# Even mixer of a two-layer decoder trunk: index scores in groups beside x_b, gate units in blocks beside nine pairs of the attention, LRU factors on Pool

## The chip, the cores and the metric

The kernel is one program on one core of a Trainium2 chip. The core has five engines that run their own instruction streams and meet only at semaphores: TensorE (PE in the profile; PEld is its weight load), VectorE (DVE), ScalarE (ACT), GpSimd (POOL) and SyncE (SP, which here only issues transfers). The metric is the device time of one launch in microseconds (us), lower is better.

## The reference

The trunk works on h (512 tokens x 1024 channels, float32). Each of two layers adds a half-step FFN, a mixer, a cross-attention to 256 memory tokens and a second half-step FFN. The change lies in the mixer of layer 0, the even mixer:

```python
q, c_kv, q_i, k_i, w_i, gate_b, x_b = _split(h @ w_in, EVEN_SPLITS)   # 512,256,512,64,8,512,512
c_kv = rmsnorm(c_kv, kv_norm); k = c_kv @ w_uk; v = c_kv @ w_uv       # 8 heads of 64
# index scores, 8 index heads of 64; the top 128 keys of each query are kept
sc = einsum('bqhd,bsd->bqhs', q_i, k_i) * IDX_DIM ** -0.5
score = where(causal, einsum('bqhs,bqh->bqs', relu(sc), w_i * IDX_HEADS ** -0.5), -inf)
_, idx = top_k(score, 128)
a_out = softmax over the kept keys of (q @ k^T * 64 ** -0.5), times v
# RG-LRU on the other 512 channels
xc = causal_dwconv(x_b, conv_w, conv_b)                               # 4 taps
r = sigmoid(xc @ w_ra + b_ra); i = sigmoid(xc @ w_ri + b_ri)
log_a = -8 * r * softplus(-lam); a = exp(log_a)
b = sqrt(-expm1(2 * log_a)) * (i * xc)
b_out = scan(h_t = a_t * h_{t-1} + b_t) * gelu(gate_b)
return concat([a_out, b_out]) @ w_out
```

## The kernel before

Weights come as a stream of units of 128 x 1024 float32 (512 KB). SP loads unit v into one of two raw buffers when unit v-2 has been split; ACT writes the rounded high part (`split_hi`, L334) and DVE the low part (`split_lo`, L339), and PE multiplies high by high, high by low and low by high (`three`, L354 to L356, or `streamed`, L1592 to L1594). A unit of a projection is 8 blocks of three matmuls with 512 columns. Four slots hold split units, so a split is written 4 units ahead (`AHEAD`) of the one being drained. `w_ready` counts units that are split, `w_free` those that PE has used, `p_free` projection tiles copied out of PSUM.

The order of work in `even` is written out by hand on each engine; nothing is scheduled. Before the change it is, on PE:

- q_idx, c_kv, and the unit with the index keys and weights; then 24 index scores (L1789: three query blocks of 8 heads, with 256, 384 and 512 columns, in float32, two passes each). They go to PSUM banks 2 and 3 in turn, each waiting for the `relu` (ACT, L801) of the one two before.
- x_b (4 units), uk (1), uv (1), gate (4), then 8 LRU gate products (L1814), then q (4).
- the attention (`attend`, 32 steps, 8 heads of 4 query tiles t with (t+1)*128 keys): score (L1822) into bank 0 or 1; DVE adds the selection mask `e_sc` and takes the row maximum (L1161) and scales it (L1164); ACT takes the exponential (L687); DVE multiplies by the reciprocal of the sum (L1171, L1172); PE transposes the probabilities two steps later (L1636); DVE copies them to `e_pT` (L1179); after each head PE mixes with v (L1830), ACT and DVE split the result (L705, L1148). `recurrence` puts the LRU factors, their products and the scan between these steps on DVE.
- the output projection (`output`, L1592 to L1594, 8 units).

On DVE each index score is accumulated into `e_sc` (L1287, L1291), with the norm of c_kv between (`latent`: L1256 to L1272). Then follows the selection: 48 rounds, each of MAX8 (L1305), which finds the 8 largest, and MATCH_REPLACE8 (L1306), which marks them, 16 rounds for each of the three query blocks. Four rounds stand behind each of the 14 splits from x_b to q. On Pool: one causal fill for each query block, then the convolution of the four x_b tiles (L433 to L438: one tensor_scalar and six tensor_tensor for each), then i * xc (L445).

## Time and profile before

| | us |
|---|---|
| runs of the kernel, median (lowest to highest) | 2417.82 (2417.5 to 2418.16), 3 runs |
| the profiled execution | 2417.31 |
| its span in the trace | 2415.5 |
| PE, DVE, ACT, POOL busy | 2328.6, 1024.7, 843.6, 48.0 |
| mean granted clock of TensorE | 0.97 |

The profiled execution is 0.51 us below the median; 1.8 us of it lie outside the span. Times in the trace count from the start of the span. "Granted clock" is the share of full speed that TensorE was given: 1.00 is 2.4 GHz and 0.50 is 1.2 GHz. Matmuls overlap in the pipeline, so the pitch of a stream is read from the starts of its rows, not from the duration of one. The even mixer from its index scores on stands between 429 and 651 us; PE is near fully busy at full clock almost everywhere else.

### The profile page before, as it was taken

The page shows a single profiled execution, that of the slowest core. Times are in us where ns is not written, and L with a number is a line of the kernel's source. Part 1 is how long each engine was busy: PE and PEld are TensorE (multiplying, and loading weights), DVE is VectorE, ACT ScalarE, POOL GpSimd, SP SyncE. Part 2 cuts the span into 40 slices and gives each one's busy share as a digit, 9 for nine tenths or more (in the row PEclk, how much of TensorE's full clock was granted, in tenths as well). Part 3 has the DMA queues.
Part 4 walks back from the last instruction along what each step waited for, and adds up shares of the span by engine and source line. Part 5 has one row for each costly group of instructions (what it writes and reads, how often), then busy time and mean ns, then how long its engine had stood idle before and what let it go on. Part 6 is the DMA issues. An engine that isn't in the chain of part 4 may idle for free.

```text
span 2415.5 us, 28776 instructions
## 1 busy us (share of the span) xinstructions
PE 2328.6 (96%) x10808; PEld 1886.4 (78%) x10808; DVE 1024.7 (42%) x1544; ACT 843.6 (35%) x1343; POOL 48.0 (2%) x54
## 2 busy tenths in 40 slices
PE   7999999997899999999999999999988999999998
PEld 7888888573487788888888888888757877888887
DVE  4333235697563453333253333243364535333322
ACT  4222224353253443222243222244433534322321
POOL 0000000240000000000000000000000000000000
PEclk9999999796799999999999999999999999999999
DMA  4222332120134213323223223323203412233232
GB/s 157 96 96 96 105 113 83 42 78 21 44 105 131 78 63 105 100 95 109 96 87 105 96 96 106 99 86 105 84 30 105 148 63 86 87 96 100 96 101 87
DMA packets 61938, 221.83 MB, mean 92 GB/s; under 512 B 7952, under 2 KB 8080, under 8 KB 61856
## 3 DMA queue, kind: packets, MB, share of 16 engines
q1 hardware_dynamic: 57024, 207.64, 26.7%
q10 hardware_dynamic: 4832, 13.03, 1.6%
q8 instruction: 59, 0.97, 0.2%
q14 instruction: 23, 0.19, 0.0%
HBM read 218.55 MB, written 2.10 MB: 91 GB/s over the span
## 4 chain that ended last, share of the span: by engine, by line
PE 90%; DVE 7%; issue 2%; ACT 1%; DMA 0%; SPq 0%; DVEq 0%; ACTq 0%
PE ps L354 17%; PE ps L356 17%; PE ps L355 17%; PE ps L1592 10%; PE ps L1594 10%; PE ps L1593 10%; DVE e_sc L1306 1%; PE ps L1702 1%; PE ps L1711 1%; DVE e_max L1305 1%; PE ps L1493 1%; PE ps L1830 1%; DVE w_lo L339 1%; PE ps L1789 1%; PE ps L1822 0%
## 5 line engine op out<-in xcount | busy, mean ns | idle before, releaser
L354 PE MATMUL ps<-x_hi,w_hi 128*128 128x512 f32 (+1 forms) x2016 | 753.4, 374 | 11.5 <-issue 9.4
L355 PE MATMUL ps<-x_lo,w_hi 128*128 128x512 f32 (+1 forms) x2016 | 747.6, 371 | 0.0
L356 PE MATMUL ps<-x_hi,w_lo 128*128 128x512 f32 (+1 forms) x2016 | 747.4, 371 | 0.0
L339 DVE TENSOR_TENSOR w_lo<-w_raw,w_hi 128x1024 fp32r<-128x1024 f32 x194 | 242.3, 1252 | 544.9 <-ACT w_hi L334 544.0
L354 PEld LDWEIGHTS ps<-x_hi,w_hi 128*128 128x128 f32 x2016 | 383.0, 190 | 80.2 <-issue 16.1
L355 PEld LDWEIGHTS ps<-x_lo,w_hi 128*128 128x128 f32 x2016 | 383.1, 190 | 65.1 <-issue 1.2
L356 PEld LDWEIGHTS ps<-x_hi,w_lo 128*128 128x128 f32 x2016 | 382.7, 190 | 64.6
L350 DVE TENSOR_TENSOR w_lo<-w_raw,w_hi 128x1024 fp32r<-128x1024 f32 x176 | 215.8, 1226 | 291.5 <-ACT w_hi L345 291.5
L334 ACT ACTIVATE w_hi<-w_raw 128x1024 fp32r<-128x1024 f32 x194 | 204.8, 1057 | 374.5 <-PE ps L1594 304.7
L345 ACT ACTIVATE w_hi<-w_raw 128x1024 fp32r<-128x1024 f32 x176 | 186.2, 1058 | 280.8 <-PE ps L356 275.6
L1592 PE MATMUL ps<-w_hi,act_hi 128*128 128x512 f32 x608 | 236.5, 389 | 0.0
L1593 PE MATMUL ps<-w_lo,act_hi 128*128 128x512 f32 x608 | 236.5, 389 | 0.0
L1594 PE MATMUL ps<-w_hi,act_lo 128*128 128x512 f32 x608 | 236.5, 389 | 0.0
L1077 DVE TENSOR_TENSOR tmp<-ps,tmp 128x512 f32<-128x512 f32 x88 | 60.9, 692 | 315.1 <-ACT tmp L603 315.1
L603 ACT ACTIVATE tmp<-ps 128x512 f32<-128x512 f32 x88 | 52.8, 600 | 370.2 <-PE ps L356 370.2
L1592 PEld LDWEIGHTS ps<-w_hi,act_hi 128*128 128x128 f32 x608 | 114.1, 188 | 23.8
L1593 PEld LDWEIGHTS ps<-w_lo,act_hi 128*128 128x128 f32 x608 | 114.1, 188 | 23.7
L1594 PEld LDWEIGHTS ps<-w_hi,act_lo 128*128 128x128 f32 x608 | 114.1, 188 | 23.5
L1592 PE MATMUL ps<-w_hi,x_hi 128*128 128x512 f32 x192 | 76.4, 398 | 6.0 <-DVE x_lo L1462 4.5
L1593 PE MATMUL ps<-w_lo,x_hi 128*128 128x512 f32 x192 | 75.8, 395 | 0.0
L1594 PE MATMUL ps<-w_hi,x_lo 128*128 128x512 f32 x192 | 75.7, 394 | 0.0
L1081 DVE TENSOR_TENSOR act_lo<-tmp,act_hi 128x512 f32 x88 | 60.2, 684 | 0.0
(280 smaller groups left out, 2250.7 us busy)
## 6 DMA issues: line engine op xcount, KB each, us to landing
w_raw<-in_wstream SPq DMA_DIRECT2D x390, 512.0 KB, 3.5
gain_bc<-in_gains ACTq DMA_DIRECT2D x8, 512.0 KB, 4.5
tmp<-in_post_gains ACTq DMA_DIRECT2D x8, 512.0 KB, 4.5
c_mem<-in_mem ACTq DMA_DIRECT2D x2, 1024.0 KB, 4.8
out_dram<-h SPq DMA_DIRECT2D x4, 512.0 KB, 2.6
h<-in_x SPq DMA_DIRECT2D x2, 512.0 KB, 6.1
h<-in_x ACTq DMA_DIRECT2D x2, 512.0 KB, 7.5
c_gain<-in_mem_gains ACTq DMA_DIRECT2D x2, 512.0 KB, 6.0
```

The costliest lines, as they stand in the source:

```text
L334: nc.scalar.activation(weights(v)[0], w_raw[:, v % 2, :], ACT.Copy).then_inc(w_hi_ready, 1)
L339: nc.vector.tensor_tensor(wl, w_raw[:, v % 2, :], wh.bitcast(f32), ALU.subtract).then_inc(w_ready, 1)
L345: nc.scalar.activation(weights(like)[0], w_raw[:, like % 2, :], ACT.Copy).then_inc(w_hi_ready, 1)
L350: nc.vector.tensor_tensor(wl, w_raw[:, like % 2, :], wh.bitcast(f32), ALU.subtract).then_inc(w_ready, 1)
L354: nc.tensor.matmul(dst, wh, xh, start=start, stop=False)
L355: nc.tensor.matmul(dst, wh, xl, start=False, stop=False)
L356: return nc.tensor.matmul(dst, wl, xh, start=False, stop=stop)
L1077: nc.vector.tensor_tensor(tmp[:, jj, :], bank(2 * jj + 1), tmp[:, jj, :], ALU.mult)\
L1081: nc.vector.tensor_tensor(act_lo[:, bass.ds(j, 1), :], tmp[:, jj:jj + 1, :], act_hi[:, bass.ds(j, 1), :].bitcast(f32), ALU.subtract)\
L1592: nc.tensor.matmul(dst, ah, wh, start=start, stop=False)
L1593: nc.tensor.matmul(dst, ah, wl, start=False, stop=False)
L1594: return nc.tensor.matmul(dst, al, wh, start=False, stop=stop)
```

## The change

- **Unit order.** In the stream q now comes before gate. SP has ten transfers written out for this stretch, with `stream_unit` giving the place in the unchanged array, between two loops.
- **Index scores.** `IN_FRONT = (2, 6, 5, 5, 5, 5, 4)`: of the 32 blocks of x_b, so many stand before each group of four scores, and four behind the last. The scores use four banks (2, 3, 5, 6). On ACT and DVE the copies and splits that x_b brings stand after n = 3, 11, 19; on DVE three selection rounds each stand after n = 11, 15, 19, 23.
- **Selection.** The other 36 rounds stand behind the splits at x_b 3, uk, uv, q 0, q 1, q 2 (8, 6, 6, 6, 5, 5).
- **LRU.** The 8 gate products go in as 6 behind q 1 and 2 behind q 2. The five factor steps per tile (with one more instruction, six) and the two products before the scan move from DVE to Pool; Pool's fills stand between its convolutions. The gelu and the product with it stand after the attention, the square root after pair 7.
- **Attention.** 16 pairs m of two steps. The key projection is copied with scale -1/8 and the mask is +3e38 for excluded keys, so that DVE's min is the bias itself: the small scaling instruction and its wait are gone. `e_p` has six slots. The copy of the transposed probabilities goes from DVE to ACT. `BESIDE = (4, 4, 4, 4, 4, 3, 3, 3, 3)`: the 32 blocks of gate stand beside pairs 0 to 8. From pair 10 on, even pairs write banks 6 and 7, odd ones 0 and 1.
- **Output.** The first two of the 8 output units are started tile by tile (`out_tile`) while the last head and the gelu are under way.

On PE at the start of the index scores, before:

```order
L1776 MATMUL ps<-tmp,ones 128x512 [waits e_sq] x2
L1780 MATMUL ps<-ident,e_wi 128x8 [waits p_free]
L1780 MATMUL ps<-ident,e_wi 128x8 x3
L1789 MATMUL ps<-e_k,e_qi 128x256 [waits e_w]
L1789 MATMUL ps<-e_k,e_qi 128x256
L1789 MATMUL ps<-e_k,e_qi 128x256 [waits e_relu] x6
L1789 MATMUL ps<-e_k,e_qi 128x384 [waits e_relu] x8
L1789 MATMUL ps<-e_k,e_qi 128x512 [waits e_relu] x8
L354 MATMUL ps<-x_hi,w_hi 128x512 [waits w_ready,p_free]
```

The same place after (L1800 is the index score, L356 to L358 are a block of x_b):

```order
L356 MATMUL ps<-x_hi,w_hi 128x512 [waits w_ready,p_free,e_w]
L357 MATMUL ps<-x_lo,w_hi 128x512
L358 MATMUL ps<-x_hi,w_lo 128x512
L356 MATMUL ps<-x_hi,w_hi 128x512
L357 MATMUL ps<-x_lo,w_hi 128x512
L358 MATMUL ps<-x_hi,w_lo 128x512
L1800 MATMUL ps<-e_k,e_qi 128x256 [waits e_w]
L1800 MATMUL ps<-e_k,e_qi 128x256 x3
L356 MATMUL ps<-x_hi,w_hi 128x512
```

Blocks of x_b now stand before and between the scores, and the first four scores wait for no relu.

On DVE in the accumulation of the index scores, before:

```order
L1287 TENSOR_SCALAR e_sc<-tmp,e_w 128x384 [waits e_relu,stat_link]
L1291 SCALAR_TENSOR_TENSOR e_sc<-tmp,e_w,e_sc 128x384 [waits e_acc,e_relu] x2
L1267 SCALAR_TENSOR_TENSOR e_ck<-e_ck,col,e_t 128x512
L1291 SCALAR_TENSOR_TENSOR e_sc<-tmp,e_w,e_sc 128x384 [waits e_acc,e_relu] x3
```

The same place after (L1301 and L1302 are a selection round, L341 the low part of a weight unit):

```order
L1313 TENSOR_SCALAR e_sc<-tmp,e_w 128x384 [waits e_relu,stat_link]
L1317 SCALAR_TENSOR_TENSOR e_sc<-tmp,e_w,e_sc 128x384 [waits e_acc,e_relu] x2
L1277 SCALAR_TENSOR_TENSOR e_ck<-e_ck,col,e_t 128x512
L1317 SCALAR_TENSOR_TENSOR e_sc<-tmp,e_w,e_sc 128x384 [waits e_acc,e_relu]
L341 TENSOR_TENSOR w_lo<-w_raw,w_hi 128x1024 [waits w_hi_ready]
L1301 MAX e_max<-e_sc 128x8 [waits e_filled]
L1302 MATCH_REPLACE e_sc<-e_max,e_sc 128x256 [waits stat_link]
L1301 MAX e_max<-e_sc 128x8 [waits stat_link]
```

A split and three rounds now stand between accumulations; the first round waits for Pool's fill, which stands behind Pool's first convolution.

On PE in the attention, before (L1822 score, L1636 transposition, L1830 mix):

```order
L1822 MATMUL ps<-e_kT,e_qT 128x256 [waits at_sm]
L1636 MATMUL ps<-ident,e_p 128x128 [waits at_pT,at_p]
L1636 MATMUL ps<-ident,e_p 128x128 x3
L1822 MATMUL ps<-e_kT,e_qT 128x384 [waits at_sm]
L1636 MATMUL ps<-ident,e_p 128x128 [waits at_pT,at_p]
L1830 MATMUL ps<-e_pT,e_v 64x512 [waits at_pT]
```

After, around pair 0 (L1844 is the score):

```order
L1844 MATMUL ps<-e_kT,e_qT 128x128 [waits e_sig,p_free]
L1844 MATMUL ps<-e_kT,e_qT 128x256
L356 MATMUL ps<-x_hi,w_hi 128x512 [waits w_ready,p_free]
L357 MATMUL ps<-x_lo,w_hi 128x512
L358 MATMUL ps<-x_hi,w_lo 128x512
L356 MATMUL ps<-x_hi,w_hi 128x512
```

Scores stand in pairs, and four blocks of gate stand between a pair's scores and the transpositions of the pair before.

The diff, cut to its core:

```diff
-    "even": [("q_idx", 4), ("c_kv", 2), ("kw_idx", 1), ("x_b", 4), ("uk", 1), ("uv", 1), ("gate", 4), ("q", 4),
+    "even": [("q_idx", 4), ("c_kv", 2), ("kw_idx", 1), ("x_b", 4), ("uk", 1), ("uv", 1), ("q", 4), ("gate", 4),
...
+        gate_bank = (2, 3, 4, 5, 6, 7, 2, 3)
+        index_bank = (2, 3, 5, 6)
+        NOT_CAUSAL, TAKEN, MASKED = -3.4e38, -3.2e38, 3.0e38
+
+        IN_FRONT = (2, 6, 5, 5, 5, 5, 4)
+        BESIDE = (4, 4, 4, 4, 4, 3, 3, 3, 3)
...
+        def score_bank(step):
+
+            m = step // 2
+            return bank((6 if m > len(BESIDE) and m % 2 == 0 else 0) + step % 2)
...
+                conv(0)
+                fill(1)
+                conv(1)
+                fill(2)
+                conv(2)
+                fill(3)
+                conv(3)
                 for c in range(LRUT):
-                    pool.wait_ge(e["sig"], 2 * LRUT)
-                    nc.gpsimd.tensor_tensor(e_xc[:, c, :], e_xc[:, c, :], f_i[:, c, :], ALU.mult)\
-                        .then_inc(e["t2"], 1)
+                    T, R, Z = f_r[:, c, :], tmp[:, c, :], e_t[:, c % 2, :]
+                    pool.wait_ge(e["sig"], LRUT + c + 1)
+                    nc.gpsimd.tensor_tensor(e_xc[:, c, :], e_xc[:, c, :], f_i[:, c, :], ALU.mult).then_inc(e["t2"], 1)
+                    pool.wait_ge(e["tanh"], c + 1)
+                    link(nc.gpsimd.tensor_scalar(R, R, 0.5, 0.5, ALU.mult, ALU.add))
+                    link(nc.gpsimd.tensor_tensor(Z, T, R, ALU.mult))
+                    link(nc.gpsimd.tensor_tensor(Z, Z, R, ALU.add))
+                    link(nc.gpsimd.tensor_scalar(Z, Z, -1.0, 2.0, ALU.mult, ALU.add))
+                    link(nc.gpsimd.tensor_tensor(R, R, Z, ALU.mult))
+                    pool.wait_ge(e["t2"], c + 1)
+                    nc.gpsimd.tensor_scalar(f_i[:, c, :], R, 2.0, -1.0, ALU.mult, ALU.add).then_inc(e["bv"], 1)
+                for c in range(LRUT):
+                    pool.wait_ge(e["sqrt"], c + 1)
+                    link(nc.gpsimd.tensor_tensor(tmp[:, c, :], f_r[:, c, :], tmp[:, c, :], ALU.mult))
+                    nc.gpsimd.tensor_tensor(e_xc[:, c, :], tmp[:, c, :], e_xc[:, c, :], ALU.mult)\
+                        .then_inc(e["prod"], 1)
...
+                    if n % 8 == 3:
+                        project_one("x_b", n // 8, e_xb, CONV - 1)
+                project_one("x_b", 3, e_xb, CONV - 1)
...
+                for m in range(N // 2 + 1):
+                    if m < N // 2:
+                        for step in (2 * m, 2 * m + 1):
+                            c, w = step % 4 * 4, (step % TT + 1) * P
+                            act.wait_ge(at_sm, a0 + step + 1)
+                            nc.scalar.activation(e_p[:, step % 6, 0:w], e_p[:, step % 6, 0:w], ACT.Exp,
+                                                 bias=e_st[:, c:c + 1], scale=-1.0,
+                                                 accum_out=e_st[:, c + 2:c + 3]).then_inc(at_e, 1)
+                    if m < len(BESIDE):
+                        done = [sum(BESIDE[:n]) // UB for n in (m, m + 1)]
+                        for j in range(*done):
+                            project_one("gate", j, e_gate)
+                    if m == 7:
+                        act.preload_act_table(ACT.Sqrt)
                         for c in range(LRUT):
+                            act.wait_ge(e["bv"], c + 1)
                             nc.scalar.activation(f_r[:, c, :], f_r[:, c, :], ACT.Sqrt, scale=4.0)\
                                 .then_inc(e["sqrt"], 1)
                         act.preload_act_table(ACT.Exp)
-                    c, k = divmod(step - 13, 5)
-                    if k == 3 and 0 <= c < LRUT:
-                        act.wait_ge(e["y"], c + 1)
-                        nc.scalar.activation(x_hi[:, 4 + c, :], e_xc[:, c, :], ACT.Copy).then_inc(e["y_hi"], 1)
-
-                attend(i, AH, e_p, e_st, AD ** -0.5, even_slots, 1, lambda t: t + 1, False, recurrence_steps)
+                    if m in (10, 11, 14):
+                        upper_out({10: 0, 11: 1, 14: 2}[m])
...
+                            g, t = divmod(step, TT)
+                            act.wait_ge(at_t, a0 + step + 1)
+                            nc.scalar.activation(e_pT[:, g % 2, 0:t + 1, t * P:(t + 1) * P],
+                                                 bank(2 + step % 2)[:, 0:(t + 1) * P]
+                                                 .rearrange("p (k c) -> p k c", k=t + 1), ACT.Copy).then_inc(at_pT, 1)
+                act.preload_act_table(ACT.Gelu_apprx_tanh)
+                upper_out(3)
+                for c in range(LRUT):
+                    nc.scalar.activation(e_gate[:, c, :], e_gate[:, c, :], ACT.Gelu_apprx_tanh).then_inc(e["gelu"], 1)
+                for c in range(LRUT):
+                    act.wait_ge(e["y"], c + 1)
+                    nc.scalar.activation(x_hi[:, 4 + c, :], e_xc[:, c, :], ACT.Copy).then_inc(e["y_hi"], 1)
...
+                def take(n):
+
+                    for r in range(rounds[0], rounds[0] + n):
+                        b = r // per
+                        sc = e_sc[:, b, 0:(b + 2) * P]
+                        if r % per == 0:
+                            dve.wait_ge(e["filled"], b + 1)
+                        link(nc.vector.max(e_max8[:, :], sc))
+                        link(nc.vector.match_replace(sc, e_max8[:, :], sc, TAKEN))
+                        if r % per == per - 1:
+                            link(nc.vector.tensor_scalar(sc, sc, TAKEN, MASKED, ALU.not_equal, ALU.mult))
+                    rounds[0] += n
...
+                    if n % 8 == 3:
+                        split_units(i, "x_b", 1, n // 8)
+                    if n >= 11 and n % 4 == 3:
+                        take(3)
+                for seg, q, n in (("x_b", 3, 8), ("uk", 0, 6), ("uv", 0, 6), ("q", 0, 6), ("q", 1, 5), ("q", 2, 5)):
+                    split_units(i, seg, 1, q)
+                    take(n)
...
+                for m in range(N // 2 + 1):
+                    if m < N // 2:
+                        for step in (2 * m, 2 * m + 1):
+                            c, t = step % 4 * 4, step % TT
+                            w = (t + 1) * P
+                            dve.wait_ge(at_s, a0 + step + 1)
+                            if step >= 6:
+                                dve.wait_ge(at_t, a0 + step - 5)
+                            nc.vector.tensor_tensor_reduce(
+                                out=e_p[:, step % 6, 0:w], in0=score_bank(step)[:, 0:w],
+                                in1=e_tri[:, :] if t == 0 else e_sc[:, t - 1, 0:w], scale=1.0, scalar=MASKED,
+                                op0=ALU.add, op1=ALU.min, accum_out=e_st[:, c:c + 1]).then_inc(at_sm, 1)
+                    if m >= 1:
+                        for step in (2 * m - 2, 2 * m - 1):
+                            c, w = step % 4 * 4, (step % TT + 1) * P
+                            dve.wait_ge(at_e, a0 + step + 1)
+                            link(nc.vector.reciprocal(e_st[:, c + 3:c + 4], e_st[:, c + 2:c + 3]))
+                            nc.vector.tensor_scalar(e_p[:, step % 6, 0:w], e_p[:, step % 6, 0:w], e_st[:, c + 3:c + 4],
+                                                    None, ALU.mult).then_inc(at_p, 1)
+                    if m == 0:
+                        split_units(i, "q", 1, 3)
+                    if m < len(BESIDE):
+                        done = [sum(BESIDE[:n]) // UB for n in (m, m + 1)]
+                        for j in range(*done):
+                            split_units(i, "gate", 1, j)
+                    if m in (10, 11, 14):
+                        lower_out({10: 0, 11: 1, 14: 2}[m])
+                    if m in (10, 11, 12, 13):
+                        scan(m - 10)
+                lower_out(3)
...
+                def blocks(seg, first, n):
+
+                    for q in range(first, first + n):
+                        j, b = divmod(q, UB)
+                        u, t = U[i, seg] + j, PT0[i, seg] + j
+                        if b == 0:
+                            pe.wait_ge(p_free, t + 1)
+                            pe.wait_ge(w_ready, u + 1)
+                        wh, wl = weights(u)
+                        at = slice(b * P, (b + 1) * P)
+                        last = three(proj_bank(i, t), wh[:, at], wl[:, at], x_hi[:, b, :], x_lo[:, b, :],
+                                     b == 0, b == UB - 1)
+                        if b == UB - 1:
+                            last.then_inc(w_free, 1)
+
                 for n in range((TT - 1) * IH):
+                    if n % 4 == 0:
+                        blocks("x_b", sum(IN_FRONT[:n // 4]), IN_FRONT[n // 4])
                     b, hd = n // IH + 1, n % IH
                     p0 = hd % 2 * ID
-                    if n >= 2:
-                        pe.wait_ge(e["relu"], n - 1)
-                    nc.tensor.matmul(bank(2 + n % 2)[:, 0:(b + 1) * P], e_qi[p0:p0 + ID, hd // 2, b * P:(b + 1) * P],
+                    if n == 0:
+                        pe.wait_ge(e["w"], 1)
+                    if n >= 4:
+                        pe.wait_ge(e["relu"], n - 3)
+                    nc.tensor.matmul(bank(index_bank[n % 4])[:, 0:(b + 1) * P],
+                                     e_qi[p0:p0 + ID, hd // 2, b * P:(b + 1) * P],
                                      e_k2[p0:p0 + ID, 0:(b + 1) * P], start=True, stop=True).then_inc(e["s"], 1)
-                project(i, "x_b", 4, x_hi, x_lo)
+                blocks("x_b", sum(IN_FRONT[:-1]), IN_FRONT[-1])
...
+                for m in range(N // 2 + 1):
+                    if m < N // 2:
+                        score(2 * m)
+                        score(2 * m + 1)
+                    else:
+                        pe.wait_ge(at_olo, o0 + 2)
+                        out_tile(0, 2)
+                    if m >= 3 and m % 2 == 1:
+                        mix((m - 3) // 2)
+                    if m < len(BESIDE):
+                        blocks("gate", sum(BESIDE[:m]), BESIDE[m])
+                    if m >= 1:
+                        turn(2 * m - 2)
+                        turn(2 * m - 1)
+                out_tile(0, 3)
+                pe.wait_ge(at_olo, o0 + 3)
+                out_tile(0, 0)
+                mix(AH - 1)
+                pe.wait_ge(at_olo, o0 + 4)
+                out_tile(0, 1).then_inc(w_free, 1)
+                for t in range(TT):
+                    last = out_tile(1, t)
+                last.then_inc(w_free, 1)
                 pe.wait_ge(e["y_ready"], LRUT)
-                output(i, "out", KT // 2, x_hi, x_lo)
+                output(i, "out", KT // 2, x_hi, x_lo, done=2)
```

## Rows read from the trace of the kernel before

**Rows 1.** Busy time per stretch: stretch, its length, engines, granted clock, transfers.

```profile
core 0: us, PE busy (x) PEld busy (x) DVE busy (x) ACT busy (x) POOL busy (x), PEclk, DMA share, GB/s
429.00:458.50 29.50, 25.94 (x49) 10.59 (x49) 20.30 (x31) 13.70 (x27) 0.91 (x2) 0.53 0.06 18
458.50:543.80 85.30, 84.63 (x353) 66.98 (x352) 74.14 (x153) 40.63 (x54) 42.72 (x33) 0.98 0.23 73
543.80:549.90 6.10, 0.92 (x4) 0.52 (x4) 5.89 (x11) 2.34 (x2) 0.00 (x0) 0.74 0.04 15
549.90:600.00 50.10, 41.97 (x100) 17.75 (x101) 39.21 (x132) 17.34 (x44) 0.00 (x0) 0.64 0.07 21
600.00:650.40 50.40, 40.22 (x105) 16.86 (x103) 34.12 (x105) 13.04 (x34) 0.00 (x0) 0.72 0.00 0
775.00:825.00 50.00, 48.95 (x210) 37.19 (x208) 16.94 (x39) 18.12 (x44) 0.00 (x0) 1.00 0.18 57
```

**Rows 2.** Groups on DVE, 429 to 461 us: line, operation, count, busy, mean, idle before.

```profile
L1291 DVE SCALAR_TENSOR_TENSOR e_sc<-tmp,e_w,e_sc 128x256 f32<-128x256 f32 (+2 forms) x21 | 13.0, 617 | 8.0 <-ACT tmp L801 7.3
L1260 DVE RECIPROCAL e_t<-tmp 128x512 f32<-128x512 f32 x1 | 3.3, 3346 | 0.0
```

**Rows 3.** Groups on DVE, 461 to 549.9 us: selection rounds and weight splits.

```profile
L1305 DVE MAX8 e_max<-e_sc 128x8 f32<-128x256 f32 (+2 forms) x48 | 26.8, 558 | 1.2
L1306 DVE MATCH_REPLACE8 e_sc<-e_max,e_sc 128x256 f32<-128x256 f32 (+2 forms) x48 | 26.0, 543 | 0.0
L339 DVE TENSOR_TENSOR w_lo<-w_raw,w_hi 128x1024 fp32r<-128x1024 f32 x14 | 22.3, 1599 | 7.7 <-ACT w_hi L334 7.2
L1306 DVE MATCH_VALUE_LOAD e_sc<-e_max,e_sc 128x8 f32 x48 | 4.4, 92 | 1.7
```

**Rows 4.** Chain that ended last, at the selection's two ends: start, length, what.

```profile
466.12 1.06 ACT w_hi L334
...
549.95 0.20 DVE e_p L1161
```

**Rows 5.** Timelines of POOL and of DVE: start, duration, engine, line, operation.

```profile
467.19 1.04 POOL L436 TENSOR_TENSOR tmp<-e_xb,col 128x512 f32<-128x512 f32 x1
468.30 2.15 POOL L438 TENSOR_TENSOR e_xc<-e_xc,tmp 128x512 f32<-128x512 f32 x1
...
467.20 2.10 DVE L339 TENSOR_TENSOR w_lo<-w_raw,w_hi 128x1024 fp32r<-128x1024 f32 x1 [7.25 <-ACT w_hi L334]
...
504.74 1.23 DVE L339 TENSOR_TENSOR w_lo<-w_raw,w_hi 128x1024 fp32r<-128x1024 f32 x1
```

**Rows 6.** Timeline of PE: gate products, first scores, one mix, a later score.

```profile
514.33 7.03 PE L1814 MATMUL ps<-e_xc,e_bd 128*128 128x512 f32 x16
...
543.82 0.92 PE L1822 MATMUL ps<-e_kT,e_qT 64*128 64x128 f32 x4 [0.69 <-ACT e_qT L670]
...
587.07 4.33 PE L1830 MATMUL ps<-e_pT,e_v 128*64 128x512 f32 x8
591.34 1.12 PE L1822 MATMUL ps<-e_kT,e_qT 64*128 64x512 f32 x2
```

**Rows 7.** Waits, 549.9 to 651 us: who for whom, total, times, longest.

```profile
ACT e_p L687 <- DVE e_st L1164: 57.5, 27, 5.0
PEld ps L1636 <- DVE e_p L1172: 29.9, 24, 2.2
```

**Rows 8.** Groups on ACT and DVE in the attention, 549.9 to 651 us.

```profile
L687 ACT ACTIVATE e_p<-e_p,e_st 128x128 f32<-128x128 f32 (+3 forms) x32 | 17.9, 561 | 57.6 <-DVE e_st L1164 57.5
L844 ACT ACT_TABLE_LOAD x1 | 1.3, 1283 | 0.0
...
L1353 DVE TENSOR_TENSOR_SCAN e_t<-f,e_t 128x512 f32<-128x512 f32 x4 | 4.9, 1213 | 0.0
```

**Rows 9.** Timeline at the end of the attention.

```profile
649.77 0.60 ACT L705 ACTIVATE x_hi<-ps 128x512 fp32r<-128x512 f32 x1 [5.97 <-PE ps L1830]
...
651.15 0.50 PE L1592 MATMUL ps<-w_hi,x_hi 128*128 128x512 f32 x1 [1.41 <-DVE x_lo L1148]
```

329 lines of the change are left out of this document (122 added, 207 removed).

## The prediction

> **What bounds the kernel now.** I read the page's 40 slices first: apart from the start, PE's busy share and clock fall clearly in the slices of the even mixer alone, so only there can a new order of the same work gain. Then busy time by stretch [rows 1], where the reader is to see four different limits. From 429 to 458.5 us PE runs the 24 index scores at clock 0.53, with DVE waiting 8 us between its accumulations [rows 2]. From 458.5 to 543.8 PE is full (84.63 of 85.30 us, clock 0.98) with projections. From 543.8 to 549.9 PE stands still, because the third attention score needs DVE, and DVE is still selecting. From 549.9 to 650.4 come the 32 attention steps at clock 0.64 and 0.72: PE waits for normalised probabilities, ACT for DVE's maxima [rows 7]. No engine is full there; it is a chain of small hand-overs. The next output matmul starts at 651.15 [rows 9].
>
> **One chain on DVE.** The first accumulation ends its wait at about 430.4, and the selection ends at 549.95 [rows 4]: 119.5 us. So the first question is what DVE must still do before the attention in the new order.
>
> - 24 accumulations: 13.0 us for 21 of them [rows 2], with the three first ones and 0.06 us between neighbours 16.0.
> - the norm of c_kv: the reciprocal is 3.3 [rows 2], the six other 512-wide operations about 0.7 each: 7.6.
> - 48 rounds: 26.8 + 26.0 + 4.4 busy and 2.9 between [rows 3] is 60.1, with three closing operations 61.4. A round is 0.98 us at 256 keys, 1.25 at 384, 1.5 at 512.
> - 9 splits instead of 14 (gate's four and q's last are moved behind): 9 x 1.23 [the undisturbed one in rows 5] = 11.1.
>
> Sum 96.1. Waits that remain: DVE follows the first scores and ACT's table load to about 435, then the split behind n = 3 needs the first x_b tile. That is 8 blocks and four scores after 429.1: 8 x 0.68 (55.8 us from 458.5 to 514.33 [rows 6] for 80 blocks, less 1.4 of cold clock) and 1.8, so 436.4; copy 0.6 and high part 1.06 [rows 4] make 438.0. Together about 4.4 us of waits. Behind that the relus are ahead of DVE: four banks, and PE needs at most 3.4 + 3.4 us for five blocks and four scores, where DVE needs 6 to 8 for its four accumulations, rounds and split. **Without anything else the selection would end at 430.4 + 96.1 + 4.4 = 530.9**, 19 us earlier.
>
> **What Pool does to it.** In the trace a DVE operation with two inputs in SBUF and Pool's tensor_tensor take turns. At 467.20 the split starts as Pool's product does, and takes 2.10 instead of 1.23; Pool's next one takes 2.15 instead of 1.3, because it waits for the split [rows 5]. The 14 splits have a mean of 1.60 [rows 3], so some 5 us are lost now. Before the change the accumulations, which also read two SBUF tiles, met no convolution. Now the first three convolutions (0.77 + 3 x 1.04 + 3 x 1.29 + gaps = 8.3 us each, and 0.08 us from one instruction to the next) start with each x_b tile and fall among them. I walked the two orders against each other, letting each wait out the other's instruction: in the first convolution the split and three accumulations are held (3.4 us), in the second the split, two accumulations and a c_kv product (3.7), in the third the split and three accumulations (3.4), later four splits (2.5). **Sum 13 us, so the attention starts on DVE at about 544.** The ends of this cost are 0 (only splits suffer as now: 5 us) and 24 accumulations at 1.04 (25 us). MAX8 and MATCH_REPLACE8 have one input, and the trace shows them undisturbed beside Pool, which is why I take the walk. The Trainium skill, SBUF — State Buffer, section "Who interferes with whom", says that the pair of ports shared by the two engines is an exclusive lock, held for the whole instruction, also for a DVE instruction with two SBUF inputs. By that rule the walk's alternation holds; rows 5 agree (2.10 against 1.23).
>
> PE needs from 429.1: 32 blocks 21.8, scores at full clock some 17, uk and uv 10.9, q 21.8, the gate products 7 [rows 6], some 6 of waits for copies, and 4 blocks of gate: done near 520 to 525. So **PE stands still for some 20 us before the second pair**, instead of 6 now. Moving gate away from here buys nothing here; what it buys is cover later. Pool's factors (six instructions and the product with i, 8.0 us a tile, from the first tanh near 517 on) end near 549, before the square roots ask for them.
>
> **The attention.** At full clock, for one head (two pairs): its mix is half of 4.33 [rows 6], 2.2; scores 2.6 (the same 2560 columns in two passes, and weight loads); transpositions 1.2.
>
> - Pairs 1 to 8: 4 x 2.6 + 3 x 2.2 + 4 x 1.2 + 28 blocks x 0.68 = 41 us of PE, which is the slowest engine here: DVE has 2 to 3.3 us a pair, ACT 2.3 to 4, against 3.8 to 7.2. The cross-attention, woven in the same way, shows PE at 48.95 of 50 us and clock 1.00 [rows 1]. PE comes in cold after its 20 us still: +3.
> - Pair 7 puts two table loads (1.28 each [rows 8]) and four square roots (0.6) between ACT's exponentials and the copies on which PE's transpositions wait: 5 us of ACT, of which I let 4.5 through.
> - Pairs 9 to 15 have no blocks. Odd ones are PE's: scores 1.85, mix 2.2, transpositions 0.4, 4.5 with hand-overs. Even ones are the chain score, minimum, two normalisations (0.49 and 0.42 with a reciprocal each), transposition: 3.4, and 0.5 more with a scan of 1.21 [rows 8] in front. Sum 30. At half clock the odd ones would be 8, the even ones 4.4. PE's share is 74% here, between the 43% of now (clock 0.68) and the cross-attention's; I add 5.
> - The end: pair 16, the last mix, and the two output units that stand in for waiting. Counting the eight tiles (1.36 each) back from their end, the output starts, in effect, 5 us after pair 15. The gelu chain (four at 0.6, copies, low parts) ends some 6.5 us after the last mix; the tiles behind it last 8.4. It stays hidden.
>
> 41 + 3 + 4.5 + 30 + 5 + 5 = 88.5. **The output starts, in effect, at 544 + 88.5 = 632.5 instead of 651.15: 18.6 us less.** Behind it nothing changes: the memory load is issued some 8 us later relative to the output, and PE needs it only in the second half, 25 us on. SP's ten written transfers keep the same waits. 2417.31 - 18.6 = 2398.7 in the profiled execution, 2399 on the median.
>
> **The rivals.**
>
> 1. *Pool costs little.* DVE wins more of the turns, or the accumulations drift out of the convolutions. Then the attention starts near 531 and the output at 620: 31 us less, 2387; with the clock full to the end 2382. Against it stands the alternation in rows 5.
> 2. *The clock stays low in pairs 9 to 16.* All at half: 4 x 8 + 3 x 4.4 = 45 instead of 35, and some 2 at the end: 12 us dearer, 2411. For it: now the stretch shows 0.64 to 0.72 [rows 1].
> 3. *The selection gains nothing.* If contention costs its upper end, DVE ends at or after 549.9, and only the attention gains: 12 us or less, 2406 to 2412. This is also how the change could fail to do what it says: the gate units left a stretch that DVE bounds.
> 4. *Slower.* PE does not regain its clock in pairs 1 to 8, since each block group is followed by transpositions that wait for DVE and ACT. At half clock throughout, 41 becomes 82 and pairs 9 to 16 cost 12 more: 53 dearer, 2452. It decides when about half of pairs 1 to 8 runs at half clock (18.6 of the 41 us that all of it would add). Against it is the clock of 1.00 in the cross-attention [rows 1]. The Trainium skill, TensorE: Matmul & The Clock Gate, Part 1, puts it so that the default is throttled and activity releases it; by that rule, too, dense blocks keep the clock.
>
> **How the numbers follow.** The forecast has 0.50, rival 1 0.22, rival 2 0.12, rival 3 0.08, rival 4 0.08. The likeliest is 2399. From 2381 (rival 1 with a full clock) to 2412 (rivals 2 and 3) holds some 0.85; the bounds of the contention, 5 and 25 us instead of 13, lie within it (2391 and 2411). A measurement of this kernel tells about 0.2%, 5 us, from no change: faster 0.89, same 0.03, slower 0.08.
>
> **What the profile after would show.** DVE's first attention operation near 544 (531 for rival 1); accumulations with durations near 1.7 us among those of 0.5 to 0.75, and Pool's of 1.8 to 2.2 beside them; PE idle for some 20 us before the second pair; clock 1.00 from there to pair 9 and mixed behind; the last mix near 635; the second-half output without a wait for memory. It would be wrong by the size of the contention first, by the clock in the last seven pairs second, and by ACT at pair 7 third.

## The result, and the profile after

| | before | after |
|---|---|---|
| median (lowest to highest), 4 runs each | 2417.66 (2417.22 to 2418.16) | 2394.61 (2391.14 to 2396.57) |
| the profiled execution | 2417.31 | 2394.80 |
| its span in the trace | 2415.5 | 2393.1 |
| PE, DVE, ACT, POOL busy | 2328.6, 1024.7, 843.6, 48.0 | 2302.6, 1004.7, 852.7, 85.2 |

The ratio is 0.9903 (95% interval 0.9886 to 0.9920): 23 us faster. The forecast was 2399, the range 2381 to 2412.

I call a pair m from 0 on, as the change does. Busy time by stretch in the changed kernel, to be laid beside [rows 1] (stretch, length, engines, granted clock): up to the last accumulation, up to PE's standstill, the standstill, pair 1, pairs 2 to 8, pairs 9 to the last mix.

```profile
427.60:479.80 52.20, 44.87 (x158) 28.82 (x159) 40.18 (x62) 20.77 (x38) 28.66 (x23) 0.87 0.13 41
479.80:517.70 37.90, 37.90 (x147) 28.21 (x146) 36.04 (x85) 15.12 (x20) 11.22 (x10) 0.96 0.18 56
517.70:541.60 23.90, 6.45 (x19) 4.20 (x17) 22.97 (x43) 9.34 (x13) 18.85 (x18) 0.70 0.15 45
541.60:549.60 8.00, 7.66 (x19) 4.56 (x19) 6.21 (x13) 2.72 (x9) 7.58 (x8) 0.62 0.21 66
549.60:589.20 39.60, 38.32 (x163) 24.30 (x162) 19.07 (x60) 24.59 (x57) 9.41 (x8) 1.00 0.12 41
589.20:629.40 40.20, 35.82 (x119) 17.68 (x118) 24.38 (x68) 19.47 (x50) 5.08 (x4) 0.83 0.05 13
```

PE (first pair of numbers) is busy for 6.45 of 23.9 us in the third line: it stands still for 17.5 us while DVE (third pair) is full. In the fifth it is full and at full clock, where [rows 1] had 0.64. The chain that ended last says the same of the hand-over (start, length, what), to be laid beside [rows 4]:

```profile
539.68 0.67 DVE e_sc L1302
...
540.37 1.19 DVE e_sc L1304
...
541.59 0.29 DVE e_p L1350
...
541.94 3.35 PE ps L1844 x4
```

DVE's first minimum of the attention starts at 541.59 instead of 549.95. The 549.95 that the prediction calls the end of the selection is that start: in DVE's timeline before, the closing operation of the selection ends at 547.56, and two splits follow, which now stand elsewhere:

```profile
547.13 0.43 DVE L1308 TENSOR_SCALAR e_sc<-e_sc 128x512 f32<-128x512 f32 x1
547.59 2.36 DVE L339 TENSOR_TENSOR w_lo<-w_raw,w_hi 128x1024 fp32r<-128x1024 f32 x2
```

PE's timeline has its two waits in this stretch (start, duration, and in brackets the idle time in front and its releaser):

```profile
526.20 1.64 PE L1844 MATMUL ps<-e_kT,e_qT 64*128 64x128 f32 x4 [7.92 <-ACT e_qT L816]
...
541.94 3.35 PE L1844 MATMUL ps<-e_kT,e_qT 64*128 64x384 f32 x4 [9.87 <-DVE e_st L1350]
```

The groups on DVE from 430 to 480 us, beside [rows 2] and the splits of [rows 3]: the same 21 accumulations take 854 ns instead of 617, and the first three splits 1805 instead of the undisturbed 1230.

```profile
L1317 DVE SCALAR_TENSOR_TENSOR e_sc<-tmp,e_w,e_sc 128x256 f32<-128x256 f32 (+2 forms) x21 | 17.9, 854 | 2.5 <-ACT tmp L826 1.1
L341 DVE TENSOR_TENSOR w_lo<-w_raw,w_hi 128x1024 fp32r<-128x1024 f32 x3 | 5.4, 1805 | 4.6 <-ACT w_hi L336 4.6
```

The timelines of DVE and of POOL, as in [rows 5], show two accumulations of 384 keys in 2.50 us (0.62 each when alone) and a product of 1.75 (0.75 alone), each beside Pool's convolution:

```profile
458.06 2.50 DVE L1317 SCALAR_TENSOR_TENSOR e_sc<-tmp,e_w,e_sc 128x384 f32<-128x384 f32 x2
460.48 1.75 DVE L1277 SCALAR_TENSOR_TENSOR e_ck<-e_ck,col,e_t 128x512 f32<-128x512 f32 x1
...
457.55 1.28 POOL L464 TENSOR_TENSOR e_xc<-e_xc,tmp 128x512 f32<-128x512 f32 x1
458.90 1.24 POOL L462 TENSOR_TENSOR tmp<-e_xb,col 128x512 f32<-128x512 f32 x1
460.22 1.46 POOL L464 TENSOR_TENSOR e_xc<-e_xc,tmp 128x512 f32<-128x512 f32 x1
```

Waits from 541 to 633 us, beside [rows 7] (who for whom, total, times, longest). ACT's wait for DVE's minima is 31.2 us, 14 of them before the first pair, instead of 57.5; PE's for normalised probabilities 9.8 instead of 29.9:

```profile
ACT e_p L882 <- DVE e_st L1350: 31.2, 22, 14.0
...
PEld ps L1852 <- DVE e_p L1359: 9.8, 15, 1.5
DVE w_lo L341 <- ACT w_hi L336: 9.4, 4, 5.3
```

The clock is not full to the end. The mixes of [rows 6] took 4.33 us; PE's timeline now has two such behind pair 8, each in a stretch of its own at half clock (599 to 606 and 609 to 616 us), while the chain shows 2.30 us for the others:

```profile
600.83 4.53 PE L1862 MATMUL ps<-e_pT,e_v 128*64 128x512 f32 x8
605.92 0.92 PE L1844 MATMUL ps<-e_kT,e_qT 64*128 64x128 f32 x4
609.08 3.35 PE L1844 MATMUL ps<-e_kT,e_qT 64*128 64x384 f32 x4
612.36 4.11 PE L1862 MATMUL ps<-e_pT,e_v 128*64 128x512 f32 x8
```

At the end, to be laid beside [rows 9]: the last mix ends at 631.8, and the output goes on at 633.18.

```profile
631.81 0.60 ACT L875 ACTIVATE x_hi<-ps 128x512 fp32r<-128x512 f32 x1 [3.13 <-PE ps L1862]
...
633.18 0.50 PE L1606 MATMUL ps<-w_hi,x_hi 128*128 128x512 f32 x1 [1.41 <-DVE x_lo L1333]
```

Three of the early tiles are done by then (3 x 1.36 us), so the output starts, in effect, at 629.1 instead of 651.15: 22.05 us of the 22.4 by which the spans differ. Behind it both kernels need 1764 us.

One part of it is not the change's. The scale of the index weights, which ends what both kernels do alike, stands in DVE's timeline at 428.90 before and at 427.41 after; in the runs below it stands anywhere from 427.1 to 429.8. So 1.5 us of this profile's gain is chance. Of the other 20.6 us, 6.9 lie ahead of DVE's first minimum (from that row 121.0 us before and 114.2 after) and 13.7 behind it (101.2 us to the output before, 87.5 after). Where I give a distance, I count each trace from its own row of this kind:

```profile
428.90 0.18 DVE L1278 TENSOR_SCALAR e_w<-ps 128x32 f32<-128x32 f32 x1
```

```profile
427.41 0.18 DVE L1288 TENSOR_SCALAR e_w<-ps 128x32 f32<-128x32 f32 x1
```

### The profile page after: what moved, and what is told of

The parts are those of the page before. It is cut to its first block, busy times and chain, and to the rows that moved or that the text cites. A ratio compares the mean times of both kernels' runs of the same rounds, so it can differ in the third digit from the quotient of the medians.

```text
span 2393.1 us, 28715 instructions
## 1 busy us (share of the span) xinstructions
PE 2302.6 (96%) x10808; PEld 1877.4 (78%) x10808; DVE 1004.7 (42%) x1452; ACT 852.7 (36%) x1374; POOL 85.2 (4%) x86
## 4 chain that ended last, share of the span: by engine, by line
PE 91%; DVE 6%; issue 2%; ACT 1%; DMA 0%; SPq 0%; DVEq 0%; ACTq 0%
PE ps L356 18%; PE ps L357 18%; PE ps L358 18%; PE ps L1606 10%; PE ps L1607 10%; PE ps L1608 10%; DVE e_sc L1302 1%; PE ps L1694 1%; PE ps L1703 1%; DVE e_max L1301 1%; PE ps L1506 1%; PE ps L1844 1%; PE ps L1862 1%; DVE w_lo L341 1%; DVE e_sc L1317 1%
## 5 line engine op out<-in xcount | busy, mean ns | idle before, releaser
L356 PE MATMUL ps<-x_hi,w_hi 128*128 128x512 f32 (+1 forms) x2016 | 757.1, 376 | 13.4 <-issue 9.6
L358 PE MATMUL ps<-x_hi,w_lo 128*128 128x512 f32 (+1 forms) x2016 | 748.9, 371 | 0.0
L341 DVE TENSOR_TENSOR w_lo<-w_raw,w_hi 128x1024 fp32r<-128x1024 f32 x194 | 242.2, 1251 | 541.8 <-ACT w_hi L336 541.1
L356 PEld LDWEIGHTS ps<-x_hi,w_hi 128*128 128x128 f32 x2016 | 383.5, 190 | 89.4 <-issue 22.5
L358 PEld LDWEIGHTS ps<-x_hi,w_lo 128*128 128x128 f32 x2016 | 383.4, 190 | 65.2
L1606 PEld LDWEIGHTS ps<-w_hi,act_hi 128*128 128x128 f32 x608 | 114.1, 188 | 23.8
L1608 PEld LDWEIGHTS ps<-w_hi,act_lo 128*128 128x128 f32 x608 | 114.1, 188 | 23.7
L1607 PEld LDWEIGHTS ps<-w_lo,act_hi 128*128 128x128 f32 x608 | 114.1, 188 | 23.6
```

The lines of the kernel that those rows point to most:

```text
L341: nc.vector.tensor_tensor(wl, w_raw[:, v % 2, :], wh.bitcast(f32), ALU.subtract).then_inc(w_ready, 1)
L356: nc.tensor.matmul(dst, wh, xh, start=start, stop=False)
L358: return nc.tensor.matmul(dst, wl, xh, start=False, stop=stop)
L1606: nc.tensor.matmul(dst, ah, wh, start=start, stop=False)
L1607: nc.tensor.matmul(dst, ah, wl, start=False, stop=False)
L1608: return nc.tensor.matmul(dst, al, wh, start=False, stop=stop)
```

## The experiments

Each was timed against the kernel before on its own chip, so runs are compared by their ratios. "Selection" and "last mix" are the ends of the two in the profiled execution, in us from that row on. The kernel before has 118.7 and 220.8 there.

| run | median us | ratio (95%) | selection | last mix |
|---|---|---|---|---|
| changed kernel | 2394.61 | 0.9903 (0.9886 to 0.9920) | 114.1 | 204.4 |
| e1 convolution cut | 2386.54 | 0.9866 (0.9851 to 0.9881) | 104.8 | 193.8 |
| e2 convolutions late | 2388.48 | 0.9869 (0.9854 to 0.9884) | 106.1 | 195.5 |
| e3 16 gate blocks in front | 2390.18 | 0.9882 (0.9867 to 0.9898) | 114.1 | 198.3 |
| e4 no roots | 2391.83 | 0.9895 (0.9878 to 0.9912) | 112.7 | 202.5 |
| e5 plain output | 2401.99 | 0.9930 (0.9917 to 0.9944) | 112.5 | 197.2 |
| e6 gate in front | 2399.01 | 0.9913 (0.9898 to 0.9928) | 119.8 | 204.7 |
| e8 three products more | 2403.81 | 0.9940 (0.9926 to 0.9953) | 114.1 | 209.3 |
| e9 scores first | 2383.68 | 0.9847 (0.9833 to 0.9860) | 101.8 | 194.4 |
| e10 copy on DVE | 2421.87 | 1.0011 (1.0002 to 1.0020) | 114.3 | 230.9 |
| e11 factors on DVE | 2410.91 | 0.9965 (0.9953 to 0.9977) | 112.4 | 221.0 |
| e12 one product more | 2389.72 | 0.9880 (0.9865 to 0.9895) | 114.0 | 198.0 |
| e15 combined | 2374.31 | 0.9820 (0.9807 to 0.9833) | 101.6 | 181.4 |

The ends scatter by some 1.5 us: e4 and e5 change nothing ahead of the attention, and have 112.7 and 112.5. The last mix scatters by more, since the clock in the last pairs differs from trace to trace (last section).

### Does Pool's convolution hold DVE?

e1 leaves out six of seven instructions of each tile's convolution:

```diff
                         if k == 0:
-                            link(nc.gpsimd.tensor_scalar(e_xc[:, c, :], e_xb[:, c, 0:SEQ], ...))
+                            nc.gpsimd.tensor_scalar(e_xc[:, c, :], e_xb[:, c, 0:SEQ], ...).then_inc(e["conv"], 1)
+                            break
```

> The changed kernel with Pool's convolution cut to its first product: the six two-input operations a tile are left out, so the recurrence gets other values. Theory (Pool's and DVE's two-input operations take turns, and that holds DVE): in the trace of the changed kernel ten of DVE's accumulations, splits and c_kv products between 437 and 483 us are longer than alone, by 7.7 us in sum; without them DVE's selection ends near 534 instead of 541.6, and the time is 7 to 8 us lower, near 2387. Rival (DVE is held by PE's scores and ACT's relus there, which absorb what the shorter operations give back): the selection ends less than 3 us earlier, 2392 to 2395.

e2 keeps all of it and changes Pool's order alone:

```diff
-                conv(0)
-                fill(1)
-                conv(1)
-                fill(2)
-                conv(2)
-                fill(3)
-                conv(3)
+                for b in range(1, TT):
+                    fill(b)
+                for c in range(LRUT):
+                    conv(c)
```

> The changed kernel with one edit on Pool: the three causal fills first, then the four convolutions, so that none of them meets an accumulation. Theory: DVE gets back the 7.7 us that its operations are held between 437 and 483 us, but the splits at 494, 502 and 511 us now fall into the convolutions (0.9 each): the selection ends near 536.6, 5 us earlier. The convolutions end near 518, so the LRU gates run some 6 us later, and the last copy of q is done near 532, in time. Time near 2390. Rival 1 (the contention costs little): the time stays at 2394 to 2396. Rival 2 (the gates become late and with them q, the first score waits for them): 2395 or more.

The selection ends 9.3 us earlier in e1 and 8.1 in e2, and the median is 9 and 8 us lower against the kernel before. DVE's groups in e2 over the accumulation (430 to 473 us) show what was given back, against the two rows of the changed kernel above:

```profile
L1314 DVE SCALAR_TENSOR_TENSOR e_sc<-tmp,e_w,e_sc 128x256 f32<-128x256 f32 (+2 forms) x21 | 12.9, 617 | 2.5 <-ACT tmp L823 1.1
...
L341 DVE TENSOR_TENSOR w_lo<-w_raw,w_hi 128x1024 fp32r<-128x1024 f32 x3 | 3.7, 1225 | 4.3 <-ACT w_hi L336 4.3
```

The idle time in front of the accumulations is 2.5 us in both: nothing absorbs the gain, and the rival falls. That e2 gains 8 and not 5 lies in the splits: four of its nine meet a convolution, but are held 2.2 us in sum (0.4 to 0.7 each, not 0.9), while in the changed kernel the nine were held 2.9, the last two by Pool's factors, which now come too late for them. Another 1.4 us of it is not the edit's: the first accumulation waits 2.9 us in e2's trace and 4.3 in the changed kernel's, and no edit reaches that place. The later LRU gates cost nothing: the scores of pair 1 still start right behind the selection (535.74 and 536.13 us).

### What are the blocks between the scores worth?

e9 takes e2 and puts all scores in front:

```diff
-        IN_FRONT = (2, 6, 5, 5, 5, 5, 4)
+        IN_FRONT = (0, 0, 0, 0, 0, 0, 32)
...
-                for seg, q, n in (("x_b", 3, 8), ("uk", 0, 6), ("uv", 0, 6), ("q", 0, 6), ("q", 1, 5), ("q", 2, 5)):
+                for seg, q, n in (("x_b", 0, 3), ("x_b", 1, 3), ("x_b", 2, 3), ("x_b", 3, 4), ("uk", 0, 5),
+                                  ("uv", 0, 5), ("q", 0, 5), ("q", 1, 4), ("q", 2, 4)):
```

> The kernel of the run with the late convolutions, with one further edit: all 24 index scores stand ahead of all blocks of x_b, as before the change (the splits of x_b move behind the accumulations, with three or four selection rounds behind each; twelve rounds still stand between the accumulations, and banks stay four). It is read against the run with the late convolutions (0.9869 of the kernel before). Theory (DVE is full from the first score to the end of the selection in either order, and PE has idle time before the attention to absorb the clock at half during the scores): the selection ends within 2 us of that run's 535.7, PE gets q done some 5 us later, near the selection's end, and the time is 0 to 4 us higher, 0.987 to 0.989. Rival (the blocks between the scores are what frees DVE or PE): the attention starts 8 us or more later, 0.990 or above.

Neither: it is faster, by 4.3 us in the selection and 5 us in the ratio (0.9847 against 0.9869; the intervals meet). Its stretches up to the last accumulation and from there to the end of the selection:

```profile
428.00:462.20 34.20, 26.43 (x65) 14.65 (x66) 29.60 (x61) 14.54 (x28) 0.90 (x2) 0.60 0.05 16
462.20:530.40 68.20, 64.45 (x257) 49.44 (x255) 63.21 (x130) 31.09 (x41) 49.13 (x41) 0.95 0.22 70
```

PE's clock of 0.60 in the first line does no harm, because DVE sets the pace there, and in the second PE still finishes q 7 us before DVE. So weaving x_b between the scores, which looks like the heart of the change, brings nothing and seems to cost some 4 us. DVE's waits up to the end of the selection tell where: for the relu of the first accumulation 1.4 us in e9 against 2.9 in e2, for the high parts of x_b's splits 2.4 against 4.3. Over the same stretch DVE's listed waits sum to 16.4 us before the change, 10.1 in the changed kernel and 4.9 in e9, where the twelve rounds and the splits stand so that DVE has work while it would wait. The rounds' own share was not measured: no run takes them out, nor the four banks.

### What is gate's move worth?

e6 puts gate back in front of the attention on all three engines:

```diff
                 blocks("q", 3 * UB, UB)
+                blocks("gate", 0, 4 * UB)
...
-                    if m < len(BESIDE):
-                        blocks("gate", sum(BESIDE[:m]), BESIDE[m])
```

> The changed kernel with the 32 blocks of gate, their splits and copies put back in front of the attention (behind q), as in the kernel before; the nine pairs run bare. Theory of the prediction (PE stands still for some 18 us before the attention anyway, so gate costs only a few us in front, DVE's four more splits 5 us; the worth of the move is what the blocks cover in pairs 1 to 9): the attention starts 8 to 9 us later (near 550). If bare pairs run at the pace of pairs 10 to 15 of the changed kernel (27 us for six, 4.5 each), eight take 36 instead of 47.6 and the time is 2 to 3 us lower, near 2392. If they run at the pace of the kernel before (50 us for eight), the time is 11 us higher, 2405. The first says that cover is worth nothing, the second that it is worth the move.

The same edit puts q's last split ahead of the attention too, so DVE has five more splits there. The ratio is 0.9913 against 0.9903, 2.4 us, and the two intervals leave room for anything from 3 us faster to 8 slower. The last mix ends at the same distance, but e6's trace has pairs 11 and 13 at 4.5 and 6.1 us where the changed kernel's has 7.8 twice. Its stretch from the end of the selection to the scores of pair 8, without any block:

```profile
548.50:588.50 40.00, 32.16 (x86) 14.53 (x86) 17.22 (x62) 16.59 (x45) 7.78 (x7) 0.66 0.07 22
```

The clock is 0.66. Pairs 1 to 7, which are seven and not eight as I wrote in what e10 was to show, need 37.5 us bare and 42.3 covered, at full clock from pair 2 on. In exchange the selection ends 5.7 us later and, with the last split of gate behind it, DVE's first minimum stands 7.8 us later. The timelines of DVE and PE in e6:

```profile
548.61 2.16 DVE L341 TENSOR_TENSOR w_lo<-w_raw,w_hi 128x1024 fp32r<-128x1024 f32 x1
...
551.04 3.35 PE L1838 MATMUL ps<-e_kT,e_qT 64*128 64x384 f32 x4 [4.40 <-DVE e_st L1349]
```

e3 leaves half of gate beside the pairs:

```diff
-        BESIDE = (4, 4, 4, 4, 4, 3, 3, 3, 3)
+        BESIDE = (16, 2, 2, 2, 2, 2, 2, 2, 2)
```

> The changed kernel with 16 of gate's 32 blocks beside pair 0 and two beside each of pairs 1 to 8; ACT copies those two tiles before its first exponential. In the changed kernel PE stands still between 518 and 542 us except for the first scores and four blocks. Theory (pairs 1 to 8 are PE's: 42.3 us from the scores of pair 1 to those of pair 8, and blocks that move into the idle time shorten them): 12 blocks by 0.68 us leave the pairs, but the pairs without any block, as the run with gate in front showed, need 37.5 us for the same stretch, so only some 5 us come back, and the time is near 2390. It is to be read with that run, where all 32 blocks stood in front and nothing was gained, because the attention started 5.5 us later with the selection and 3 more with q. Rival (hand-overs set the pairs, whatever the blocks): within 1.5 us of the changed kernel, at the same distance from the kernel before, 0.990.

2390.18, and 5 us lower by the ratio, as expected, though the intervals meet. The selection ends when it did and the last mix 6.1 us earlier. Pairs 1 to 8 take 42.2 us instead of 47.2. Behind them pair 9 is 1.3 us longer, and pair 13 is 3.3 shorter, for which no edit stands near it.

### Where do the shorter pairs come from?

e10 gives the copy of the transposed probabilities back to DVE, behind the next pair's minima:

```diff
-                            act.wait_ge(at_t, a0 + step + 1)
-                            nc.scalar.activation(e_pT[:, g % 2, 0:t + 1, t * P:(t + 1) * P],
...
+                    if m >= 2:
+                        copies(m - 1)
```

> The changed kernel with the copy of the transposed probabilities back on DVE, behind the minima of the next pair. This asks where the shorter pairs come from, since the run with gate in front showed eight bare pairs in 37.5 us, where the kernel before needed 50. Theory (DVE's share of a pair sets the pace, the copy on ACT took two copies of 0.3 to 0.7 us a pair and a wait for PE off it): the attention takes 8 to 15 us longer, 2403 to 2410. Rival (the grouping of two steps into a pair and the direct minimum did it, the copy is only work that fits anywhere): within 3 us, 2394 to 2398.

26 us slower, more than the whole gain, and far outside my 8 to 15. The copies are only 14.3 us of DVE in all. The chain of e10 shows why they cost twice that (start, length, what):

```profile
603.66 0.55 DVE e_p L1351
604.21 0.01 DVE e_st L1351
604.22 0.60 DVE e_p L1351
604.82 0.01 DVE e_st L1351
604.83 1.08 DVE e_pT L1338 x2
...
605.95 3.41 PE ps L1866 x8
```

PE's mix waits for copies that wait behind minima that wait for PE's scores. In seven of the eight heads PE stands idle for 1.9 to 2.0 us in front of the mix, as it does in front of no mix of the changed kernel's timeline. The clock is 0.71 from 602 to 660 us, and this mix takes 3.41 us instead of 2.30. e10 prices the copy at this place in DVE's order; another place was not tried.

e11 gives the six factor instructions of each tile back to DVE, beside pairs 1 to 4:

```diff
+                    if 1 <= m <= LRUT:
+                        factors(m - 1)
```

> The changed kernel with the six factor instructions of each LRU tile back on DVE, beside pairs 1 to 4; Pool keeps the product with i and the two products before the scan. Theory: DVE gets 4 x 2.9 us more in four pairs in which it is busy for 2 to 3.3 us of 5 to 7, so it becomes the engine that PE waits for; Pool no longer holds the last splits and closing operations of the selection (2.3 us). Together 2 to 6 us slower, 2397 to 2400. Rival (it fits beside the blocks of gate): the time falls by the 2.3 us, 2392.

0.9965, 15 us slower, where I had expected 2 to 6. The selection ends 1.7 us earlier, no more than these ends scatter; pairs 1 to 5 take 46.9 us (541.6 to 588.5) instead of 31.8. DVE's groups there, which Pool had done in the changed kernel, are 13.5 us in all with three of them as follows:

```profile
L1340 DVE TENSOR_TENSOR tmp<-tmp,e_t 128x512 f32<-128x512 f32 x4 | 2.8, 693 | 0.1
...
L1339 DVE TENSOR_SCALAR e_t<-e_t 128x512 f32<-128x512 f32 x4 | 1.7, 426 | 0.1
L1342 DVE TENSOR_SCALAR f<-tmp 128x512 f32<-128x512 f32 x4 | 1.7, 426 | 0.1
```

Here the loss is about what the work takes. Yet DVE is idle half of the time there: in the changed kernel it is busy for 19.07 of the 39.6 us of pairs 2 to 8, in e11 for 22.56 of 38.5 (550.0 to 588.5 us), where PE's clock is 0.78. What DVE does in a pair stands in line with what PE waits for, so idle time elsewhere does not hide it.

### The clock in the last pairs

e8 adds three products of 512 columns beside each of pairs 10 to 15, e12 one beside pairs 10, 12 and 14 (e12's diff):

```diff
+                    if m in (10, 12, 14):
+                        pe.wait_ge(at_sm, a0 + 2 * m)
+                        for k in range(1):
+                            nc.tensor.matmul(score_bank(2 * m - 2), e_qT[:, 0, 0:P], e_kT[:, 0, :], ...)
```

> The changed kernel with three more matrix products of 512 columns beside each of pairs 10 to 15 (their result is not used). There the trace of the changed kernel shows the clock at half in two stretches, from 598.9 to 605.7 and from 609.1 to 615.9 us, with mixes of 4.46 and 4.04 us instead of 2.3. Theory (the low clock in these stretches costs some 5 us, and a busier PE keeps it full): the clock is 1.00 up to the last mix, and the time 2 to 5 us lower, since the added products take about 0.5 us each partly in idle time. Rival (PE's idle time there is not what lowers the clock, or the pairs are set by hand-overs in which the filler stands in the way): the time is 0 to 6 us higher.

> The changed kernel with one added matrix product of 512 columns beside pairs 10, 12 and 14 alone (0.85 us each at full clock, as the run with three beside each of six pairs showed; the result is not used). In that run the clock was 1.00 to the end, but PE was full and the time higher. Here pairs 10, 12 and 14 take 3.2 us of which PE's own work at full clock is 1.85, so one product fits. Theory: where the clock then stays at 1.00, an odd pair takes 4.5 instead of 7.8 us, and the time falls by up to 6.6 us (0.9875). Rival (one product is too little, the clock falls all the same): the time stays within 1.5 us of the changed kernel, 0.9900 to 0.9910.

In e8 the clock is 1.00 to the end, but the products fill PE (45.02 of 46.10 us) and the kernel is 9 us slower: its work exceeds what it saves. A product takes 0.85 us there, not the 0.5 that I had entered. In e12 one product of 0.85 us in each pair in which PE waits anyway is enough (1.05 to 1.07 us in front of the transpositions in the changed kernel's timeline). Stretch of e12, and its mix in the place of the one of 4.53 us above:

```profile
594.90:602.50 7.60, 7.55 (x29) 3.52 (x28) 6.14 (x19) 5.15 (x14) 0.00 (x0) 1.00 0.00 0
```

```profile
599.74 2.37 PE L1862 MATMUL ps<-e_pT,e_v 128*64 128x512 f32 x8
```

The last mix ends 6.4 us earlier, and the ratio falls by 5.6 us, with intervals that meet: that is the price of the low clock in the last pairs. A single trace could be chance here, as one of the two stretches is missing in others as well. But from pair 11 to pair 15 the clock is 1.00 in all three traces with added products (e8, e12, e15) and in none of the ten without, where it is 0.66 to 0.91.

### The roots and the early tiles

e4 leaves out the roots and the two table loads of pair 7:

```diff
-                    if m == 7:
-                        act.preload_act_table(ACT.Sqrt)
...
-                        act.preload_act_table(ACT.Exp)
```

> The changed kernel without the four square roots of pair 7 and the two table loads around them (Pool's products take their input unrooted). Theory: ACT's 5 us there stand between its exponentials and the copies that PE's transpositions wait for, of which 4.5 us reach the end: 2390. Rival (the next pairs take it back, since PE has blocks of gate to do meanwhile): less than 1.5 us, 2393 to 2395.

0.9895 against 0.9903 is 2 us, less than the intervals can tell. The starts of pairs 8 and 10 are 8.5 us apart in its trace and 10.8 in the changed kernel's: 2.3 us, in between the theory and the rival.

e5 takes the early output tiles away:

```diff
-                        out_tile(0, 2)
...
-                for t in range(TT):
-                    last = out_tile(1, t)
...
+                output(i, "out", KT // 2, x_hi, x_lo)
```

> The changed kernel without the early output tiles: the first two output units stand with the others, behind the last mix and the gelu chain. Theory of the prediction (the eight tiles stand in for waiting): the last mix ends 1.8 us earlier, the chain of gelu, product, copy and low part near 636.2 us, and the output then starts there, where it starts now in effect at 629.0 (the tiles counted back). So 7 us slower than the changed kernel, 0.993 of the kernel before. Rival (PE's tiles only fill what the clock and the first waits of the output give back otherwise): 3 us or less, 0.9915 or below.

6.5 us slower, as expected. Its last mix ends 7.2 us earlier in the table, and not the 1.8 that I expected: 1.6 of it lie in the selection and 3.3 in pair 13, which this trace ran in 4.5 us. PE's timeline shows the standstill between the last mix and the output, and the first product behind it at half clock (0.77 instead of 0.50 us):

```profile
625.83 1.14 PE L1862 MATMUL ps<-e_pT,e_v 128*64 128x384 f32 x5
633.33 0.77 PE L1606 MATMUL ps<-w_hi,x_hi 128*128 128x512 f32 x1 [6.36 <-issue]
```

### All together

e15 is e9 with e12's product and with gate as follows, the copy of its first tile ahead of the first exponential:

```diff
-        BESIDE = (4, 4, 4, 4, 4, 3, 3, 3, 3)
+        BESIDE = (12, 2, 2, 2, 2, 3, 3, 3, 3)
```

> What the runs so far suggest, put together: scores first with Pool's convolutions late (0.9847 alone), 12 of gate's blocks beside pair 0 and two beside each of pairs 1 to 4, three beside pairs 5 to 8 (the copy of gate's first tile ahead of the first exponential), and one added product beside pairs 10, 12 and 14. Theory: the parts add, since each acts in its own stretch. The product gives 6.3 us as it did alone. Twelve blocks take 8.2 us, the idle time between the end of q (523 us) and the end of the selection (530.4) in the run with the scores first, and eight blocks by 0.68 us leave pairs 1 to 4, of which some 3 us come back (5 of 8.2 did with sixteen in front). Together 0.9847 less 9.3/2419, near 0.981, 2373 to 2376. Rival (fewer blocks beside pairs 1 to 4 bring the clock down there, as between pairs 8 and 10 in the run with sixteen): the front part gives nothing, 0.982 to 0.983.

2374.31, 0.9820 (0.9807 to 0.9833), the fastest here: 44 us below the kernel before and 20 below the changed one. The ratio alone lies between theory and rival, and the stretches decide: from the end of the selection to pair 9, e15 needs 43.5 us where e9 needs 46.7, at full clock, so the front part gives 3.2. Its stretches from the selection to pair 8 and from there to the last mix:

```profile
530.20:568.70 38.50, 37.05 (x152) 22.82 (x150) 24.00 (x65) 22.76 (x55) 20.71 (x18) 1.00 0.18 55
568.70:610.00 41.30, 38.86 (x153) 20.51 (x152) 27.94 (x76) 24.10 (x60) 9.92 (x8) 1.00 0.04 13
```

## Why the prediction held, and where it did not

| step | forecast | measured |
|---|---|---|
| DVE's first minimum | 544 | 541.6, or 543.1 without the 1.5 us of chance |
| PE's standstill | some 20 | 17.5 |
| pairs 1 to 8 | 48.5 | 47.3 (541.9 to 589.2) |
| pairs 9 to 15 | 35 | 35.1 (to 624.3) |
| end | 5 | 4.8 (to 629.1) |
| output starts, in effect | 632.5 | 629.1, or 630.6 without the chance |

- **The chain on DVE: right as the bound, its sum partly by luck.** The sum held to a microsecond, but three terms off against each other did that. From the row of the index weights on, the waits were forecast at 5.7 us (1.3 and 4.4) and the trace has 10.1: the first accumulation waits 4.3 us, since two blocks of x_b, at clock 0.61, now stand ahead of the scores, and the second split waits 2.2 for its high part, which I had not foreseen. The contention came out 3 us smaller. The work itself took some 93.5 us instead of 96.1; of that, 1.7 is the 16.0 that I entered for the accumulations, whose rows sum to 14.3.
- **The contention: right in kind, somewhat too large.** Forecast 13 us. By the durations, the 21 accumulations were held 4.9 us, the c_kv products 1.0, the nine splits 2.9 and the three closing operations 1.5, together 10.3. The walk had eight accumulations held, the trace has seven, by 0.6 to 1.0 us each; I had left out the closing operations and counted too much for the splits (5.1 us) and for the accumulations and products (7.9 against 5.9). e1 gives 9 us for the convolutions, and the other 1.5 of the 10.3 it leaves in place, in a split and a closing operation beside Pool's factors. The Trainium skill, SBUF — State Buffer, "Who interferes with whom", holds that one of the two waits out the other's instruction; e1, e2 and the row of 2.50 us agree. Rival 1 falls.
- **PE's standstill: right**, though its first half (7.92 us) waits for the last copy of q, which stands on ACT behind exponential and tanh; I had put all of it down to DVE. PE's terms in the prediction add up to 516 us and not to the "520 to 525" written behind them; PE ended q at 518.3 and the first four blocks of gate near 532.
- **Pairs 1 to 8: the sum right, two terms off against each other.** The roots and table loads cost some 2.3 us by e4, not 4.5. In their stead PE waited about 1 us in pair 2, for normalised probabilities that stood on DVE behind the split of the next unit, whose high part came late (the chain, below; DVE waited 9.4 us in all for such high parts). "PE is the slowest engine here" held: 38.32 of 39.6 us in pairs 2 to 8, and the 12 blocks that e3 takes away, 8.2 us of PE, shorten pairs 1 to 8 by 5.

```profile
549.88 1.06 ACT w_hi L336
550.96 1.70 DVE w_lo L341
...
553.85 0.50 DVE e_p L1359
...
554.39 0.66 PE ps L1852 x4
```

- **"Moving gate away from here buys nothing here; what it buys is cover later": wrong, and the other way round.** This is the reading that failed, though it entered no term; the prediction's own sum has nine splits in DVE's chain for fourteen. By e6 the move lets DVE's first minimum stand 7.8 us earlier, and its blocks make pairs 1 to 7 4.8 us longer. As a whole it is worth some 2 us, which the intervals cannot tell from nothing, and by e3 half of gate in front of the pairs is better than none.
- **Why the pairs are short: not said.** I had entered DVE's 2 to 3.3 us a pair as a given and not as a source of the gain. e10 (26 us) and e11 (15 us) show that DVE's small share is needed: each of the two alone gives back all that the attention gained (101.2 us from DVE's first minimum to the output before, 87.5 after). They do not show that it is the only source. What the grouping into pairs and the direct minimum are worth by themselves was not tested; with both in place, e10's attention is still slower than before.
- **Pairs 9 to 15 and their clock: right.** 5 us added, 6.4 measured by e12, so the other terms were 1.3 us too large. Rivals 2 and 4 fall: the clock was 1.00 in pairs 2 to 8, and half in two stretches behind. Rival 3 falls too, as DVE's first minimum came 8.4 us earlier.
- **The end: right.** The gelu chain stays hidden by the tiles; without them it is 6.5 us (e5).

## What to carry to other kernels

Where an engine is a full chain, look first at which of its operations take turns with another engine's: moving Pool's work by a few lines gave 8 us by the ratio, while weaving x_b between the scores brought nothing (e9) and gate between the pairs at most a little (e6). In a pipeline of short hand-overs, what sets the pace is the engine that takes part in most of them; copies of half a microsecond cost about twice their own time where they stood behind an operation that waits. And where PE waits in many small gaps, one useless product in each can be worth more than it costs, as long as it fits into the gap: here one did, three did not.

## What was not expected of the hardware

- One added product of 0.85 us in each of three pairs kept the clock at 1.00 from 594.9 to 625.4 us, where it fell to half twice without them, at 7.8 us for a pair instead of 4.5.
- In other runs one of the two stretches at half clock was missing without any edit near it: in e5 pair 13 takes 4.5 us, as in e1 and e3, and 7.8 in the changed kernel. Such a step is 3.3 us, about as much as the changed kernel's runs differ among themselves (2391.14 to 2396.57, where before had 2417.22 to 2418.16). Whether that is the cause of their spread was not tested.
- DVE's closing operation of the selection, which reads a single SBUF tile, is held by Pool too: 1.19 us in the chain above, where one of Pool's factor products runs from 540.00 to 541.27. Alone it takes 427 ns on 512 keys, as the groups on DVE in the kernel before show:

```profile
L1308 DVE TENSOR_SCALAR e_sc<-e_sc 128x512 f32<-128x512 f32 x1 | 0.4, 427 | 0.0
```
